# Band attention: VectorE copies a head's transposed probabilities ahead of the next item's bias and maximum of that head

## What is computed

```python
qh = head_rms(q.reshape(bsz, seq, B_HEADS, B_HD), qn_g)      # 8 heads of 64
kh = head_rms(k.reshape(bsz, seq, B_HEADS, B_HD), kn_g)
...
scores = jnp.einsum('bnqhd,bnkhd->bhnqk', qc, kb) * (B_HD ** -0.5)
...
scores = jnp.where(valid[None, :, None, None, :], scores + bias[None, None], -1e30)
probs = jax.nn.softmax(scores, axis=-1)
o = jnp.einsum('bhnqk,bnkhd->bnqhd', probs, vb)
```

## Time and profile before

| | us |
|---|---|
| median of 3 runs (lowest, highest) | 2684.51 (2684.07, 2687.04) |
| the profiled execution | 2682.55 |
| its span, first to last instruction | 2680.8 |
| TensorE busy | 2575.0 (96% of the span) |
| VectorE busy | 1469.8 (55%) |
| ScalarE busy | 894.2 (33%) |
| mean granted TensorE clock | 0.987 of full speed |

### The profile page before, as it was taken

The page is one execution under the profiler, slowest core; times in us unless marked ns, Lnnn a source line. Parts: engine busy times, 40 slices in busy tenths (PEclk is TensorE's granted clock), DMA queues, the critical chain, the costliest instruction groups (busy, mean ns, idle before and its releaser), DMA issues.

```text
span 2680.8 us, 32827 instructions
## 1 busy us (share of the span) xinstructions
PE 2575.0 (96%) x12744; PEld 2124.5 (79%) x12744; DVE 1469.8 (55%) x1809; ACT 894.2 (33%) x1252; POOL 1079.5 (40%) x770
## 2 busy tenths in 40 slices
PE   7999999899999899999989999999989999999997
PEld 6888887677788678888878887788878777888876
DVE  4475632366555667676742254668764423555554
ACT  5244234322322333333320022355542321444332
POOL 3453523211233488888834343333345332111111
PEclk9999999999999999999999999999999999999999
DMA  3101121111342021222242221211132311000022
GB/s 130 48 27 37 40 71 40 51 36 44 107 181 70 32 87 71 95 76 90 81 171 94 65 69 63 106 47 39 42 115 78 112 55 38 19 20 17 24 79 78
DMA packets 52887, 184.01 MB, mean 69 GB/s; under 512 B 5408, under 2 KB 9760, under 8 KB 51360
## 3 DMA queue, kind: packets, MB, share of 16 engines
q1 hardware_dynamic: 46560, 147.08, 16.5%
q10 hardware_dynamic: 6208, 35.27, 3.4%
HBM read 149.83 MB, written 32.51 MB: 68 GB/s over the span
## 4 chain that ended last, share of the span: by engine, by line
PE 79%; DVE 11%; ACT 4%; issue 4%; DMA 1%; POOL 1%; DVEq 0%; ACTq 0%; SPq 0%; POOLq 0%
PE ps L738 11%; PE ps L739 11%; PE ps L740 11%; PE ps L802 5%; PE ps L804 5%; PE ps L803 5%; PE ps L1040 5%; PE ps L1039 5%; PE ps L1041 5%; PE ps L1223 2%; PE ps L868 1%; PE ps L963 1%; PE ps L983 1%; PE ps L1213 1%; PE ps L971 1%
## 5 line engine op out<-in xcount | busy, mean ns | idle before, releaser
L571 POOL TENSOR_TENSOR derived_vectors<-w_staged 1x1 f32<-1x1 f32 x162 | 41.4, 256 | 1425.9 <-PE ps L740 723.8
L574 POOL TENSOR_TENSOR w_low<-w_staged,w_high 128x1024 fp32r<-128x1024 f32 x162 | 435.6, 2689 | 13.0
L802 PE MATMUL ps<-h_mix_high,w_high 128*128 128x512 f32 x688 | 282.1, 410 | 4.6 <-DVE z_hgrn_f L1817 4.6
L804 PE MATMUL ps<-h_mix_high,w_low 128*128 128x512 f32 x688 | 270.0, 392 | 0.0
L803 PE MATMUL ps<-h_mix_low,w_high 128*128 128x512 f32 x688 | 269.2, 391 | 0.0
L572 POOL CAST w_high<-w_staged 128x1024 fp32r<-128x1024 f32 x162 | 168.4, 1039 | 0.0
L802 PEld LDWEIGHTS ps<-h_mix_high,w_high 128*128 128x128 f32 x688 | 130.2, 189 | 30.5 <-issue 6.4
L804 PEld LDWEIGHTS ps<-h_mix_high,w_low 128*128 128x128 f32 x688 | 129.7, 188 | 28.2
L803 PEld LDWEIGHTS ps<-h_mix_low,w_high 128*128 128x128 f32 x688 | 130.2, 189 | 25.2 <-issue 1.0
L738 PE MATMUL ps<-act_high,w_high 128*128 128x512 f32 x352 | 137.9, 392 | 8.7 <-DVE square_sum L2173 8.7
L739 PE MATMUL ps<-act_low,w_high 128*128 128x512 f32 x352 | 137.7, 391 | 0.0
(11 more groups left out here) (488 smaller groups left out, 6915.6 us busy)
## 6 DMA issues: line engine op xcount, KB each, us to landing
w_staged<-weights_in SPq DMA_DIRECT2D x178, 512.0 KB, 3.6
w_staged_late<-weights_in SPq DMA_DIRECT2D x22, 512.0 KB, 4.0
gates_loaded<-gates ACTq DMA_DIRECT2D x8, 1024.0 KB, 7.7
gates<-tmp SPq DMA_DIRECT2D x16, 512.0 KB, 2.6
act_raw<-gates SPq DMA_DIRECT2D x16, 512.0 KB, 6.2
gates<-gates_staged_late SPq DMA_DIRECT2D x22, 256.0 KB, 2.0
x_in<-xT_in SPq DMA_DIRECT2D x8, 512.0 KB, 8.1
x_mid<-xT_in ACTq DMA_DIRECT2D x1, 4096.0 KB, 13.5
```

The costliest lines, as they stand in the source:

```text
L574: nc.gpsimd.tensor_tensor(w_low[:, j], w_staged[:, j], f32(w_high[:, j]), ALU.subtract).then_inc(s_split, 1)
L802: nc.tensor.matmul(ps[:, bank], wH, h1H[:, c, tok], start=(c == 0), stop=False)
L804: done = nc.tensor.matmul(ps[:, bank], wL, h1H[:, c, tok], start=False, stop=(c == DC - 1))
```

## The change

In VectorE's loop, for each head, the copy of item p's transposes now stands ahead of the bias and the maximum of item p+1. Nothing else is touched.

```diff
             for p in range(N):
                 for e in range(2):
+                    band_copied(p, e)
                     if p + 1 < N:
                         band_max(p + 1, e)
-                    band_copied(p, e)
                     if e == 0 and p >= 4 and p % 4 == 0:
                         band_block_done(p - 1)
                 band_block_inverted(p)
```

## The result

The changed kernel takes 2702.83 us, the median of 4 runs (2701.39 to 2705.19); the kernel before 2684.29 in the runs beside it (2683.02 to 2687.04). The ratio is 1.0072, with a 95% interval from 1.0059 to 1.0085: 18.5 us slower, where I had forecast 7.5 and a range that ends at 2695.5.

A forecast was written before the change was run, and what follows sets the result against it. TensorE carries 79% of the chain; after the change the 7.60 us loop through VectorE and ScalarE was to bound items. 3.8 + 1.4 + 0.5 + 0.5 + 0 + 1.3 = 7.5 us on 2684.51 gave 2692.0, range 2687.0 to 2695.5.

The forecast's parts named there:

- The direction: Whole kernel: slower than before, by 0.28%; chance of slower 0.72.
- The ring: Five-tile item: scores, transposes, copies, maxima, exponential, next scores form a loop of 7.60 us against 7.13; chance 0.75 that it decides.
- a block's first item: Five-tile first item of a block: scaling adds some 0.60 us, so 8.20 against 7.73; three of them, 1.4 us.
- links overlap: Rival: transposes-to-copy and memset steps overlap, items cost what they do now; +2 us, 2686.5; chance 0.15.
- faster: Rival: exponential stays ahead, TensorE's own work decides and its copy waits go; 11.8 us gained, 2672.7; chance 0.06.
- The shorter items: Items of four tiles and fewer: 1.3 us more together, between bounds of 0 and 2.5.
- Nothing was taken back behind the band: Behind the band: TensorE goes on with its queue, so what the band ends later the kernel ends later.
- the block's last item: Five-tile last item of a block: reciprocal and spread copy follow the last maximum, 7.90 us against 7.72; three, 0.5 us.
- the sixteenth item: Sixteenth item of the band: already has four-tile maxima with no memset, so 0 us more.
- a rival of its own: Rival: gaps before scores lower TensorE's clock, 3.5 us a fall; 2695.5 for one, 2702.5 for three; chance 0.04.
- One sign of being wrong: Profile after: the forecast is wrong if the granted clock in 515 to 720 is below 1.00.
- The first item: Very first item of the band: another 0.5 us more.

The follow-up runs named there:

- run 1: Changed kernel, with a block's reciprocal and spread copy moved to the head of the block's last item, ahead of its two copies; 2692.22 us, ratio 1.0027.
- run 2: Changed kernel, with the reciprocals written to PSUM so that the spread copy, in its new place, reads PSUM and not SBUF; 2692.17 us, ratio 1.0032.
- run 4: Kernel before, with only the first head's copy moved ahead of its maximum; 2711.48 us, ratio 1.0103.
- run 5: Kernel before, with only the second head's copy moved ahead of its maximum; 2692.3 us, ratio 1.0035.
- run 7: Changed kernel, with reciprocal, spread copy and scaling at the head of the item and one memset for both heads; 2683.32 us, ratio 0.9999.
- run 8: Kernel before, with both maxima between the two copies, one memset and bias for both heads, inverse and scaling at the item's head; 2673.89 us, ratio 0.9964.
- run 3: Kernel before, old order, with the reciprocal also waiting for GpSimd's cast, so the spread copy starts just behind the subtraction's start; 2723.77 us, ratio 1.0150.

## Why the prediction was wrong

**Right, by its steps.** The direction. The ring: 7.60 forecast, 7.62 measured, in each ordinary item of this kernel and of runs 1 and 2; 8.20 for a block's first item, 8.22 where the clock was full. The rivals "links overlap" and "faster" are out by the same rows. The shorter items, 1.3 forecast and 1.4 measured without their block ends. Nothing was taken back behind the band. And the same rows gave the orders of runs 4, 5, 7 and 8 to within 0.1 us an ordinary item.

**The step that failed** is the block's last item, put at 7.90 us: "the spread copy follows after 0.22 and takes 0.43". I took a duration from one neighbourhood and used it in another. In the kernel before the spread copy starts at 539.39, 0.42 ahead of GpSimd's cast; the change moves it from 5.98 us behind the start of scores to 6.79. TensorE's last filler sets off GpSimd's work, and that moved the other way, since the waits ahead of it had gone: GpSimd's first row comes 5.53 us in and not 6.03. The subtraction starts 1.24 behind it, at 6.77, just when the copy comes. My own sum had the copy at 5.82 + 0.74 + 0.22 = 6.78 and the filler's end at 5.29; GpSimd's rows were in the trace of the kernel before and I hadn't laid them beside it:

```profile
539.44 0.43 POOL L571 TENSOR_TENSOR derived_vectors<-w_staged 1x1 f32<-1x1 f32 x1 [31.94 <-PE ps L804]
...
539.81 1.03 POOL L572 CAST w_high<-w_staged 128x1024 fp32r<-128x1024 f32 x1
...
540.92 2.37 POOL L574 TENSOR_TENSOR w_low<-w_staged,w_high 128x1024 fp32r<-128x1024 f32 x1
```

A block end took 10.03 us at full clock where the sum had 7.90: three of them cost 6.9 us in place of 0.5, and two shorter ones another 1.0, where the sixteenth item had a term of 0. Runs 1, 2 and 3 show that it is this collision.

A warning stood in the same trace, just behind the band. VectorE's subtraction at 712.37 took 2.57 us beside GpSimd's; the next two of its kind, with GpSimd idle, took 1.21 each:

```profile
711.45 2.40 POOL L574 TENSOR_TENSOR w_low<-w_staged,w_high 128x1024 fp32r<-128x1024 f32 x1
...
712.37 2.57 DVE L1754 TENSOR_TENSOR o_hgrn_low<-o_hgrn,o_hgrn_high 128x1024 fp32r<-128x1024 f32 x1
```

**A second step was too low by its consequence**: the clock had a rival of its own, but tied to the gaps in front of the scores. Those were harmless, as runs 1 and 2 show (clock 1.00 from 530 to 622, with the loads of the scores idle for 1.24 us in an ordinary item and 1.35 in a block's first). It was at the 3 us gaps of the collision that the clock fell, and that cost 3.4 us. The price of one fall, 3.5 in the rival, was 2.2 and 1.3. The rival's upper number, 2702.5, lies beside the measured 2702.83 by luck: it stood for three falls at 3.5 each, and two falls at a lower price and a collision that it didn't have add up to about the same. One sign of being wrong did come true: the granted clock from 515 to 720 was 0.97.

**The first item**, put at 0.5 more without a sum of its own, took 1.9 more in the profile. With the low clock ending as early as before, run 7 has 8.89; with it ending later, runs in the old order have 9.34 and 9.46. So by these few executions about 1.1 belongs to how long the clock stayed low, the rest to the order. What decides how long it stays low is open.

## What to carry to other kernels

To move an instruction on one engine is to move it against every other engine: list what the others run at its new time, those too that share no semaphore with it, before its old duration is used. Where an instruction only has to be done some time in an item, put it where its engine waits anyway. And for an order of work, add up the ring that each engine closes; it gave every ordinary item here to 0.1 us, and it says when the whole is TensorE's own.

## What the runs showed of the hardware

A copy on VectorE from SBUF to SBUF (128 x 512 fp32, 0.43 us) doesn't run beside GpSimd's tensor operations of 128 x 1024: where it comes second it lasts until 0.28 us behind the end of the subtraction (after: 544.88 and 544.60; run 3: 543.52 and 543.24), and shows as a long row with no idle time and no releaser. It goes the other way as well: GpSimd's one-element operation, 0.18 us elsewhere, took 0.43 in the kernel before while the spread copy ran (539.44, beside 539.39 in the earlier trace rows). Copies and reductions that read PSUM were not held up: beside GpSimd's cast the copy of probabilities keeps its 0.81 (run 4, 544.75) and a maximum its 0.82 (after, 541.32), and the spread copy takes 0.69 beside the subtraction in run 2. The Trainium skill, "SBUF — State Buffer", section "Who interferes with whom", states this: VectorE and GpSimd share one pair of SBUF ports, copies in a two-port mode take it for the whole instruction, and whoever comes second is fully blocked. By that page I should have looked for it; the runs here agree in both directions. The 0.28 us are less than the copy's own 0.43; whether a part of it ran beside GpSimd's or GpSimd's rows end too late, no run shows.

TensorE's clock was at 1.00 through items with an idle 1.2 us before each scores. It fell at two of three gaps of 3 us (after) and at all eight gaps of up to 3.7 us (run 3). At the three block ends of run 4, where TensorE waited 1.3 us for a copy and 1.4 us for the spread copy, it fell at one, and once more 10 us later. Which gap brings it down stays open.
